# Index scores summed by GpSimd instead of VectorE, and the two short query blocks put in front

## The chip, the cores and the metric

The kernel runs on one core of one Trainium2 chip. The metric is the device time of one execution in microseconds. A core has a tensor engine (PE), VectorE (DVE), ScalarE (ACT), GpSimd (POOL) and SyncE (SP), which issues transfers; each takes its own instructions in order, and they meet only at semaphores.

## The reference, cut to what matters

Two transformer layers on 1024 tokens of width 1024. The change touches one part of the first: sparse attention with an indexer, beside a banded window attention. For each block of 128 queries:

```python
dots  = einsum('bqhd,bsd->bqhs', iq, ik) * 64 ** -0.5        # 8 index heads
score = einsum('bqh,bqhs->bqs', iw, relu(dots))              # summed over the heads
score = where(key_pos <= t, score, -1e30)
_, idx = top_k(score, 256)                                   # 256 keys of each query
logits = ql . c_kv[idx] + bias;  p = softmax(logits);  o = p . c_kv[idx]   # 8 heads
```

Block b sees (b + 1) x 128 keys. Blocks 0 and 1 have at most 256 and need no selection.

## The kernel before, in words

The attention stage is a list of slots (n, i), A_SLOTS: n counts query blocks in the order of ORDER, i the eight heads. In slot g = 8n + i every engine does its part of a pipeline: the tensor engine the logits of g + 1, the transposes of g - 1 and the values of g - 2; VectorE the bias and the maximum of g; ScalarE the exponentials of g. `shared_jobs` adds smaller products that share psum banks, at their places in a slot: window attention of block n + 1 (`a_log` in slots 0 to 3, `a_t`, `a_out`), the index dots of block n + 2 (`ix`, one slot ahead of their sum), the latent queries, the output of block n - 1 in slot 2, and the 24 modulation products of the second layer (`ada`, 1 MB of weights each, loaded by SyncE into two buffers).

The selection for a block is a search by bits for the 256th score, 32 rounds on VectorE. Round 0 (`pick_side`) chooses the side by the sign, each of the next 31 (`pick_bit`) counts the scores above a limit over the whole row (line 1997), compares the count (1999) and changes a bit of the limit (2002); the last one is followed by `pick_mask`, eight wider operations, of which three wide ones (scan, product, difference) take two tensors. The tensor engine adds the mask to the logits, so the first logits of a block wait for it. `pick_rounds` says which rounds stand in which slot; the first half of them comes before the window scores (`window_scores`, line 2046) and the reciprocal of the slot's exponentials (2111), the second behind.

Before the change the order is 1, 7, 6, 5, 4, 3, 2, 0. VectorE also sums the index heads (`index_sum`, lines 2077 and 2080): one operation per head, which multiplies a head's dots by its weight and adds them. Two buffers RL hold the dots of two heads. Block 7, the first with a selection, has its 32 rounds in the 15 slots from (-1, 0) to (0, 6); later blocks have 4 in each slot from (n - 2, 7) to (n - 1, 6). GpSimd makes the causal fill (`causal`, 2691) and multiplies the window's exponentials by their reciprocals (2701).

Of the kernel before, what the change touches and what calls it, by code (L numbers as in the profile page):

```python
# [16 lines left out]
P = 128  # L17
# [6 lines left out]
NH = 8  # L24
# [49 lines left out]

ORDER = (1, 7, 6, 5, 4, 3, 2, 0)
A_SLOTS = [(n, i) for n in range(-1, NT + 1) for i in range(NH) if NH * n + i <= NH * NT + 2]
BITS = 32
FIRST_ROUNDS = (2,) * 13 + (3, 3)
PLACES = ("first", "out", "query0", "banded", "ix0", "ix1", "turned", "ada", "query1")
# [6 lines left out]

ADA_SLOTS = [(-1, i) for i in (1, 3, 5, 7)] + [(0, i) for i in range(NH)] + [(n, i) for n in range(1, 7) for i in (4, 5)]


def pick_rounds(n, i):  # L90

    g = NH * n + i + NH
    if g < len(FIRST_ROUNDS):
        a = sum(FIRST_ROUNDS[:g])
        return 1, a, a + (FIRST_ROUNDS[g] + 1) // 2, a + FIRST_ROUNDS[g]
    m, r = (n + 2, 0) if i == NH - 1 else (n + 1, 4 * i + 4)
    return (m, r, r + 2, r + 4) if picking(m) else None


def shared_jobs(n, i):  # L100

    m, k, h, jobs = n + 1, n + 2 + (i + 1) // NH, (i + 1) % NH, {}
    if i == 2 and n >= 1:
        jobs["first"] = ("d_out", n - 1)
    if i == 7 and 0 <= m < NT:
        jobs["out"] = ("a_out", m, 0)
    if i < 3 and 0 <= n < NT:
        jobs["out"] = ("a_out", n, i + 1)
    if 0 <= m < NT and i < 4:
        jobs["banded"] = ("a_log", m, i)  # L110
    if 0 <= m < NT and i >= 6:
        jobs["turned"] = ("a_t", m, i - 6)
    if i < 2 and 0 <= n < NT:
        jobs["turned"] = ("a_t", n, i + 2)
    if k >= 2 and picking(k):
# [23 lines left out]

EARLY_BANKS, LATE_BANKS, EARLY_END, LATE_AT = (7, 5, 3), (7, 5, 3), 7, 5 * NH + 1  # L140
U_BANK, U_AT, U_COUNT, U_EARLY = {}, {}, {3: 0, 5: 0, 7: 0}, {}
# [11 lines left out]
def build_program(nc, I, out):  # L153
    with ExitStack() as ctx:
# [529 lines left out]
        def _(pe):  # L684
# [151 lines left out]
            pe.wait_ge(f_free, FT["memT"])  # L836
            b = ORDER[1]
            for h in range(NH):
# [76 lines left out]
            def sparse_logits(g):  # L915
                n = g // NH
                freed(("query", n, 0))
                freed(("query", n, 1))
                if g == NH + 1:
                    pe.wait_ge(u_free[3], U_EARLY[3])  # L920
                if g >= 2:
                    pe.wait_ge(s("d_e"), g - 1)
                else:
                    pe.wait_ge(s("ix0_e"), NH - 1 + g)
                L = (ORDER[n] + 1) * P
                if picking(n):
                    pe.wait_ge(s("picked"), n)
                for a in range(0, L, BW):
                    z = min(L, a + BW)
                    o = PS[:, 2 * (g % 2) + a // BW, 0:z - a]  # L930
                    ins = pe.matmul(o, lhsT=QL[:, g % NH, :], rhs=cT[:, a:z], start=True, stop=not picking(n))
                    if picking(n):
                        ins = pe.matmul(o, lhsT=ident_h[:, :], rhs=MSK[:, n % 2, a:z], start=False, stop=True)
                ins.then_inc(s("d_l"), 1)

            def sparse_transposes(g):
                pe.wait_ge(s("d_n"), g + 1)
                if g >= 1:
                    pe.wait_ge(s("d_te"), g)
                if g == NH:  # L940
                    pe.wait_ge(u_free[5], U_EARLY[5])
# [405 lines left out]
        def _(act):  # L1347
# [157 lines left out]
            def empty_shared(job):  # L1505
# [18 lines left out]
                elif kind == "ix":  # L1524
                    k, h, c = job[1:]
                    a, z = BW * c, min((ORDER[k] + 1) * P, BW * c + BW)
                    i = NH * (k - 1) + h
                    if i >= 2:
# [8 lines left out]

            L = (ORDER[1] + 1) * P
            for h in range(NH):
# [329 lines left out]
        def _(dve):  # L1869
# [125 lines left out]
            def pick_bit(b, w, v):  # L1995
# [5 lines left out]
                if b > 0:  # L2001
                    mark(dve.scalar_tensor_tensor(limit_i, limit_i, 1 << (b - 1), over_i, ALU.bitwise_xor, ALU.bitwise_xor))
                else:
                    mark(dve.tensor_tensor(limit_i, limit_i, over_i, ALU.bitwise_xor))

            def pick_mask(m, w, v):
# [11 lines left out]
                settled()  # L2018
                if m >= 3:
                    dve.wait_ge(s("d_l"), NH * (m - 1))  # L2020
                dve.tensor_tensor(MSK[:, m % 2, 0:w], above[:, 0:w], equal[:, 0:w], ALU.subtract).then_inc(s("picked"), 1)

            def pick(m, first, last):
# [3 lines left out]
                for i in range(first, last):  # L2027
                    if i == 0:
                        dve.wait_ge(s("ix_c"), m)
                    settled()  # L2030
# [35 lines left out]

            def index_sum(k, h):
                b = ORDER[k]
                L, i = (b + 1) * P, NH * (k - 1) + h
                if k == 1:  # L2070
                    dve.wait_ge(s("ix0_e"), h + 1)
                else:
                    for c in range((L - 1) // BW + 1):
                        job = ("ix", k, h, c)
                        dve.wait_ge(u_free[U_BANK[job]], U_AT[job] + 1)
                if h == 0:
                    dve.tensor_scalar(score[:, k % 2, 0:L], RL[:, 0, 0:L], iwt[:, b, 0:1], None, ALU.mult).then_inc(s("ix_s"), 1)
                else:
                    dve.wait_ge(s("ix_s"), i)
                    dve.scalar_tensor_tensor(score[:, k % 2, 0:L], RL[:, h % 2, 0:L], iwt[:, b, h:h + 1], score[:, k % 2, 0:L],  # L2080
                                             ALU.mult, ALU.add).then_inc(s("ix_s"), 1)

            for h in range(NH):
                index_sum(1, h)
            dve.wait_ge(s("attn_in"), 16 * 7)
            mark(dve.tensor_tensor(bias[:, NH:2 * NH, :], bias[:, NH:2 * NH, :], over_last(far, 2 * P), ALU.subtract))
            settled()
            for n, i in A_SLOTS:
# [8 lines left out]
                if 0 <= g < NH * NT:  # L2097
                    dve.wait_ge(s("d_lb"), g + 1)
                    dve.tensor_reduce(nmd[:, i:i + 1], pair, AX.X, ALU.max, negate=True).then_inc(s("d_m"), 1)
                if n >= 0 and picking(n + 2):  # L2100
                    index_sum(n + 2, i)
                if i == 4 and 0 <= m < NT:
# [546 lines left out]
        def _(pool):  # L2649
# [38 lines left out]
            def causal(m):  # L2688
                pool.wait_ge(s("ix_s"), NH * m)
# [4 lines left out]
            causal(1)  # L2694
            for m in range(NT):
                if m >= 2 and picking(m):
                    causal(m)
# [183 lines left out]
```

## Time and profile before

| | us |
|---|---|
| median of 3 runs | 3418.36 (3418.05 to 3422.99) |
| the profiled execution: its time | 3422.59 |
| its span, first to last instruction | 3420.8 |
| tensor engine busy | 3109.7 (91%) |
| VectorE busy | 1399.1 (41%) |
| ScalarE busy | 918.0 (27%) |
| GpSimd busy | 815.5 (24%) |

Shares over the whole span mix stages with different limits; they say little on a change in one stage. The page's 40 slices show the attention stage: from about 250 to 780 us VectorE's digit is 8 or 9, elsewhere 1 to 5. The rows below are of that stage.

### The profile page before, as it was taken

The page shows a single profiled execution, that of the slowest core. Times are in us where ns is not written, and L with a number is a line of the kernel's source. Part 1 is how long each engine was busy: PE and PEld are TensorE (multiplying, and loading weights), DVE is VectorE, ACT ScalarE, POOL GpSimd, SP SyncE. Part 2 cuts the span into 40 slices and gives each one's busy share as a digit, 9 for nine tenths or more (in the row PEclk, how much of TensorE's full clock was granted, in tenths as well). Part 3 has the DMA queues.
Part 4 walks back from the last instruction along what each step waited for, and adds up shares of the span by engine and source line. Part 5 has one row for each costly group of instructions (what it writes and reads, how often), then busy time and mean ns, then how long its engine had stood idle before and what let it go on. Part 6 is the DMA issues. An engine that isn't in the chain of part 4 may idle for free. (4 is left out here: it accounts for less than half of the span.)

```text
span 3420.8 us, 40871 instructions
## 1 busy us (share of the span) xinstructions
PE 3109.7 (91%) x16622; PEld 2516.2 (74%) x16622; DVE 1399.1 (41%) x2837; ACT 918.0 (27%) x1571; POOL 815.5 (24%) x330
## 2 busy tenths in 40 slices
PE   5987888876799979999999989999969999999997
PEld 4864555556768878888888847888759788888886
DVE  4048888963421453222222354123553432222226
ACT  3223444452222221111111142014431411211211
POOL 3110000004211133333333333231111222322223
PEclk9996888898999989999999999999989999999999
DMA  5223101011131111111111131100031121111112
GB/s 128 65 75 112 46 18 38 26 39 62 63 104 37 26 56 38 49 49 49 49 49 49 37 132 50 50 28 15 15 105 50 50 56 50 49 49 47 44 45 98
DMA packets 178761, 187.76 MB, mean 55 GB/s; under 512 B 24732, under 2 KB 147484, under 8 KB 178237
## 3 DMA queue, kind: packets, MB, share of 16 engines
q1 hardware_dynamic: 169696, 174.05, 16.4%
q10 hardware_dynamic: 8924, 11.74, 1.0%
q8 instruction: 100, 1.64, 0.2%
q14 instruction: 41, 0.33, 0.0%
HBM read 172.09 MB, written 13.68 MB: 54 GB/s over the span
## 5 line engine op out<-in xcount | busy, mean ns | idle before, releaser
L2659 POOL TENSOR_TENSOR weights_parts<-weights,weights_parts 128x2048 fp32r<-128x2048 f32 (+3 forms) x97 | 436.4, 4499 | 1159.1 <-ACT weights_parts L1369 1159.1
L732 PE MATMUL psum<-x_cols_parts,weights_parts 128*128 128x512 f32 x1552 | 609.0, 392 | 23.4 <-POOL weights_parts L2659 13.2
L734 PE MATMUL psum<-x_cols_parts,weights_parts 128*128 128x512 f32 x1552 | 607.2, 391 | 0.0
L734 PE MATMUL psum<-weights_parts,region_parts 128*128 128x512 f32 (+1 forms) x1120 | 410.2, 366 | 0.0
L732 PEld LDWEIGHTS psum<-x_cols_parts,weights_parts 128*128 128x128 f32 x1552 | 293.8, 189 | 87.5 <-issue 12.0
L732 PE MATMUL psum<-weights_parts,region_parts 128*128 128x512 f32 x864 | 337.4, 391 | 6.9 <-DVE region_parts L2613 5.8
L734 PEld LDWEIGHTS psum<-x_cols_parts,weights_parts 128*128 128x128 f32 x1552 | 293.5, 189 | 61.3
L1369 ACT ACTIVATE weights_parts<-weights 128x2048 fp32r<-128x2048 f32 (+2 forms) x98 | 181.8, 1855 | 580.8 <-DMA region<-in_bup_h_dram 142.6
L733 PE MATMUL psum<-weights_parts,region_parts 128*128 128x512 f32 x864 | 337.1, 390 | 0.0
L732 PE MATMUL psum<-weights_parts,x_cols_parts 128*128 128x256 f32 (+1 forms) x832 | 241.1, 290 | 29.5 <-POOL wide_parts L2706 12.3
L733 PE MATMUL psum<-wide_parts,weights_parts 128*128 128x512 f32 x616 | 241.0, 391 | 0.0
L733 PE MATMUL psum<-weights_parts,x_cols_parts 128*128 128x256 f32 (+1 forms) x832 | 240.1, 289 | 0.0
L734 PEld LDWEIGHTS psum<-weights_parts,region_parts 128*128 128x128 f32 x1120 | 212.6, 190 | 34.0
L732 PEld LDWEIGHTS psum<-weights_parts,region_parts 128*128 128x128 f32 x864 | 162.9, 189 | 41.5 <-DVE region_parts L2613 6.3
L733 PEld LDWEIGHTS psum<-weights_parts,region_parts 128*128 128x128 f32 x864 | 162.8, 188 | 33.8
L732 PEld LDWEIGHTS psum<-weights_parts,x_cols_parts 128*128 128x128 f32 x832 | 162.5, 195 | 30.9 <-issue 21.8
L733 PE MATMUL psum<-extra_parts,weights_parts 128*128 128x512 f32 x456 | 178.9, 392 | 0.0
L1997 DVE TENSOR_SCALAR_CACHE_REDUCE rows<-x_cols,rows 128x1024 bf16<-128x1024 f32 (+5 forms) x186 | 175.0, 941 | 3.3
L2236 DVE TENSOR_TENSOR x_rows<-x_rows,psum 128x512 f32<-128x512 f32 x112 | 77.0, 687 | 212.1 <-PE psum L734 212.1
L733 PEld LDWEIGHTS psum<-weights_parts,x_cols_parts 128*128 128x128 f32 x832 | 162.6, 195 | 0.0
L734 PE MATMUL psum<-weights_parts,wide_parts 128*128 128x256 f32 (+1 forms) x544 | 156.8, 288 | 0.0
L2602 DVE TENSOR_SCALAR region<-region 128x1024 f32<-128x1024 f32 x22 | 17.9, 815 | 318.4 <-ACT region L1846 305.0
(371 smaller groups left out, 5171.2 us busy)
## 6 DMA issues: line engine op xcount, KB each, us to landing
weights<-in_ada_w_dram SPq DMA_DIRECT2D x24, 1024.0 KB, 5.2
weights<-in_ffn_up_w_dram SPq DMA_DIRECT2D x42, 512.0 KB, 4.5
weights<-in_w_up_dram SPq DMA_DIRECT2D x16, 1024.0 KB, 5.1
weights<-in_w_down_dram SPq DMA_DIRECT2D x16, 1024.0 KB, 5.0
weights<-in_m_in_w_dram SPq DMA_DIRECT2D x12, 1024.0 KB, 5.3
weights<-in_ffn_down_w_dram SPq DMA_DIRECT2D x10, 1024.0 KB, 5.1
weights<-in_xa_wkv_dram SPq DMA_DIRECT2D x4, 2048.0 KB, 8.2
weights<-in_m_in_w_dram SPq DMA_DIRECT2D x3, 2048.0 KB, 8.3
```

Of the source, the lines that this page charges most:

```text
L732: pe.matmul(o, lhsT=a_hi, rhs=b_hi, start=(first and i == 0), stop=False)
L733: pe.matmul(o, lhsT=a_hi, rhs=b_lo, start=False, stop=False)
L734: m = pe.matmul(o, lhsT=a_lo, rhs=b_hi, start=False, stop=(last and i == len(terms) - 1))
L1369: act.activation(WHI[buf][:, 0:width], WRAW[buf][:, 0:width], ACT.Copy).then_inc(s("w_hi"), 1)
L1997: mark(dve.tensor_scalar(above[:, 0:w], v, limit, None, ALU.is_ge, ALU.add, accum_out=cnt))
L2236: dve.tensor_tensor(v, v, PS[:, 4 + (TT["down"] + m) % 4, :], ALU.add).then_inc(t_free, 1)
L2602: dve.tensor_scalar(dst, src, k[:, 1:2], k[:, 3:4], ALU.mult, ALU.add).then_inc(s("taps"), 1)
L2659: pool.tensor_tensor(WLO[buf][:, 0:width], WRAW[buf][:, 0:width], WHI[buf][:, 0:width], ALU.subtract).then_inc(s("w_lo"), 1)
```

## The change

GpSimd sums the index heads of blocks 6 to 2, in two operations per head (a multiplication in place in RL, then an addition); VectorE keeps those of block 7. The order becomes 1, 0, 7, 6, 5, 4, 3, 2. Block 7's rounds spread over 23 slots, one in each of block -1, two in each of block 1 and in the first of block 0, then one. Later blocks' rounds stand in slots (n - 1, 0) to (n - 1, 6), as 5, 5, 5, 5, 4, 4, 4, and none in slot 7. The modulation products move to slots of n = -1, 0, 1 and 6. The bit step of a round becomes an operation with one tensor and a pointer to one number.

```diff
-ORDER = (1, 7, 6, 5, 4, 3, 2, 0)
+ORDER = (1, 0, 7, 6, 5, 4, 3, 2)
+FIRST = 2
-FIRST_ROUNDS = (2,) * 13 + (3, 3)
+ROUNDS = (5, 5, 5, 5, 4, 4, 4, 0)
+FIRST_ROUNDS = (1,) * 8 + (2,) * 9 + (1,) * 6
-ADA_SLOTS = [(-1, i) for i in (1, 3, 5, 7)] + [(0, i) for i in range(NH)] + [(n, i) for n in range(1, 7) for i in (4, 5)]
+ADA_SLOTS = sorted([(n, i) for n in (-1, 1) for i in (1, 3, 5, 7)] + [(n, i) for n in (0, 6) for i in range(NH)])
...
-        return 1, a, a + (FIRST_ROUNDS[g] + 1) // 2, a + FIRST_ROUNDS[g]
-    m, r = (n + 2, 0) if i == NH - 1 else (n + 1, 4 * i + 4)
-    return (m, r, r + 2, r + 4) if picking(m) else None
+        return FIRST, a, a + (FIRST_ROUNDS[g] + 1) // 2, a + FIRST_ROUNDS[g]
+    m, a = n + 1, sum(ROUNDS[:i])
+    return (m, a, a + (ROUNDS[i] + 1) // 2, a + ROUNDS[i]) if picking(m) else None
...
-EARLY_BANKS, LATE_BANKS, EARLY_END, LATE_AT = (7, 5, 3), (7, 5, 3), 7, 5 * NH + 1
+EARLY_BANKS, LATE_BANKS, EARLY_END, LATE_AT = (7, 5, 3), (7, 5, 3), FIRST * NH - 1, 6 * NH + 1
...
-                    mark(dve.scalar_tensor_tensor(limit_i, limit_i, 1 << (b - 1), over_i, ALU.bitwise_xor, ALU.bitwise_xor))
+                    mark(dve.tensor_scalar(limit_i, limit_i, 1 << (b - 1), over_i, ALU.bitwise_xor, ALU.bitwise_xor))
...
-                if n >= 0 and picking(n + 2):
-                    index_sum(n + 2, i)
...
+            def index_sum(k, h):
+
+                b = ORDER[k]
+                L, at = (b + 1) * P, NH * (k - FIRST) + h
+                v, u = score[:, k % 2, 0:L], RL[:, h % 2, 0:L]
+                for c in range((L - 1) // BW + 1):
+                    job = ("ix", k, h, c)
+                    pool.wait_ge(u_free[U_BANK[job]], U_AT[job] + 1)
+                if h == 0:
+                    if k >= FIRST + 2:
+                        pool.wait_ge(s("picked"), k - FIRST - 1)
+                    pool.tensor_scalar(v, u, iwt[:, b, 0:1], 0.0, ALU.mult, ALU.add).then_inc(s("ix_s"), 1)
+                else:
+                    pool.tensor_scalar(u, u, iwt[:, b, h:h + 1], 0.0, ALU.mult, ALU.add).then_inc(s("ix_w"), 1)
+                    pool.wait_ge(s("ix_w"), (NH - 1) * (k - FIRST - 1) + h)
+                    pool.wait_ge(s("ix_s"), at)
+                    pool.tensor_tensor(v, v, u, ALU.add).then_inc(s("ix_s"), 1)
...
+            causal(FIRST)
+            for n, i in A_SLOTS:
+                if i == 6 and 0 <= n + 1 < NT:
+                    normalise(n + 1)
+                if n + 2 > FIRST and picking(n + 2):
+                    index_sum(n + 2, i)
+                    if i == NH - 1:
+                        causal(n + 2)
```

## Rows read from the trace of the kernel before

**Rows 1.** Windows: length, busy time of each engine (instructions), clock, DMA share, GB/s

```profile
252.80:347.98 95.18, 69.63 (x828) 42.62 (x828) 84.67 (x188) 35.66 (x105) 8.34 (x4) 0.68 0.34 109
347.98:368.04 20.06, 17.29 (x121) 8.27 (x122) 17.31 (x45) 7.04 (x19) 0.29 (x1) 0.84 0.27 91
368.04:398.43 30.39, 27.26 (x141) 16.22 (x141) 27.43 (x65) 14.94 (x24) 0.00 (x0) 0.95 0.00 1
398.43:440.11 41.68, 32.50 (x253) 20.73 (x252) 35.95 (x76) 20.99 (x46) 3.74 (x2) 0.79 0.16 51
440.11:527.08 86.97, 74.05 (x480) 47.66 (x480) 75.43 (x182) 41.88 (x86) 4.04 (x3) 0.87 0.08 25
602.94:670.57 67.63, 56.86 (x416) 38.21 (x416) 60.62 (x182) 33.51 (x78) 4.35 (x3) 0.85 0.10 32
670.57:724.57 54.00, 39.24 (x352) 27.49 (x352) 50.03 (x176) 27.32 (x70) 4.04 (x3) 0.88 0.12 40
724.57:775.91 51.34, 45.03 (x420) 33.49 (x420) 17.40 (x60) 35.11 (x118) 2.04 (x2) 0.92 0.14 23
```

**Rows 2.** Groups on VectorE: shape and count, busy us, mean ns, idle before

```profile
L2080 DVE SCALAR_TENSOR_TENSOR x_cols<-extra,rows,x_cols 128x1024 f32<-128x1024 f32 (+5 forms) x42 | 44.4, 1057 | 4.4 <-ACT extra L1530 2.3 <-ACT extra L1543 1.7
L1999 DVE TENSOR_SCALAR rows<-rows 128x1 int32<-128x1 f32 x186 | 39.8, 214 | 6.6
L2002 DVE SCALAR_TENSOR_TENSOR rows<-rows 128x1 int32<-128x1 int32 x180 | 31.2, 174 | 6.1
L2077 DVE TENSOR_SCALAR x_cols<-extra,rows 128x1024 f32<-128x1024 f32 (+5 forms) x6 | 3.5, 580 | 37.3 <-ACT extra L1543 33.4 <-ACT extra L1530 3.9
```

**Rows 3.** Groups on VectorE with shapes kept apart, of 1024 columns

```profile
L1997 DVE TENSOR_SCALAR_CACHE_REDUCE rows<-x_cols,rows 128x1024 bf16<-128x1024 f32 x31 | 39.5, 1273 | 0.4
...
L2080 DVE SCALAR_TENSOR_TENSOR x_cols<-extra,rows,x_cols 128x1024 f32<-128x1024 f32 x7 | 9.0, 1284 | 2.1 <-ACT extra L1543 1.7
```

**Rows 4.** Timeline before block 1: start, duration, engine, [idle before and releaser]

```profile
272.33 0.51 ACT L1501 ACTIVATE extra<-extra,rows 128x256 f32<-128x256 f32 x1 [6.93 <-DVE rows L2059]
...
279.69 1.89 POOL L2701 TENSOR_TENSOR extra<-extra,rows 128x1024 f32<-128x1024 f32 x1 [27.06 <-DVE rows L2065]
...
286.90 0.43 DVE L2096 TENSOR_TENSOR psum<-psum,x_cols 128x256 f32<-128x256 f32 x1
...
297.27 0.69 DVE L2046 SCALAR_TENSOR_TENSOR extra<-psum,x_cols 128x512 f32<-128x512 f32 x1 [3.23 <-PE psum L898]
```

**Rows 5.** Timeline behind block 6's mask, slots (1, 7) and (2, 0)

```profile
440.25 1.19 PE L931 MATMUL psum<-region,x_cols 128*128 128x512 f32 x1 [4.15 <-DVE mask_rows L2021]
...
446.84 0.16 DVE L2111 RECIPROCAL rows<-rows 128x1 f32<-128x1 f32 x1 [0.18 <-ACT region L1563]
...
455.39 0.69 DVE L2046 SCALAR_TENSOR_TENSOR extra<-psum,x_cols 128x512 f32<-128x512 f32 x1 [0.72 <-PE psum L872]
```

**Rows 6.** Timeline of slots (1, 4) to (1, 6): modulation products and the reciprocal

```profile
407.59 0.22 ACT L1535 ACTIVATE weights<-psum 128x64 f32<-128x64 f32 x1 [1.19 <-PE psum L905]
...
422.24 1.89 PE L905 MATMUL psum<-weights,cond 128*2 128x64 f32 x64 [0.47 <-ACT extra L1530]
...
430.20 0.16 DVE L2111 RECIPROCAL rows<-rows 128x1 f32<-128x1 f32 x1 [3.00 <-ACT region L1563]
```

**Rows 7.** Timeline of slot (2, 6), where a GpSimd product and a sum meet

```profile
508.33 3.74 POOL L2701 TENSOR_TENSOR extra<-extra,rows 128x1024 f32<-128x1024 f32 x2 [65.26 <-DVE rows L2065]
...
510.25 2.51 DVE L2080 SCALAR_TENSOR_TENSOR x_cols<-extra,rows,x_cols 128x640 f32<-128x640 f32 x1 [0.55 <-ACT extra L1530]
```

**Rows 8.** Groups on GpSimd: two tensors, and one

```profile
L2811 POOL TENSOR_TENSOR region<-region 128x1024 f32<-128x1024 f32 x22 | 52.7, 2394 | 197.9 <-ACT region L1850 192.5 <-ACT region L1834 5.4
...
L2745 POOL TENSOR_SCALAR_AFFINE_SELECT rows<-rows 36x1024 f32<-36x1024 f32 x1 | 1.1, 1087 | 0.1
```

**Rows 9.** Timeline of block 2 without rounds: two slots' maxima

```profile
742.32 0.56 DVE L2099 TENSOR_REDUCE rows<-psum 128x1 f32<-128x384 f32 x1
...
744.91 0.56 DVE L2099 TENSOR_REDUCE rows<-psum 128x1 f32<-128x384 f32 x1
```

More of the change, by code:

```diff
@@ L114, in shared_jobs @@
         jobs["turned"] = ("a_t", n, i + 2)
-    if k >= 2 and picking(k):
+    if k > FIRST and picking(k):
         jobs["ix0"] = ("ix", k, h, 0)
@@ L836, in _ @@
             pe.wait_ge(f_free, FT["memT"])
-            b = ORDER[1]
+            b = ORDER[FIRST]
             for h in range(NH):
@@ L918, in sparse_logits @@
                 freed(("query", n, 1))
-                if g == NH + 1:
+                if g == FIRST * NH + 1:
                     pe.wait_ge(u_free[3], U_EARLY[3])
@@ L926, in sparse_logits @@
                 if picking(n):
-                    pe.wait_ge(s("picked"), n)
+                    pe.wait_ge(s("picked"), n - FIRST + 1)
                 for a in range(0, L, BW):
@@ L939, in sparse_transposes @@
                     pe.wait_ge(s("d_te"), g)
-                if g == NH:
+                if g == FIRST * NH:
                     pe.wait_ge(u_free[5], U_EARLY[5])
@@ L1526, in empty_shared @@
                     a, z = BW * c, min((ORDER[k] + 1) * P, BW * c + BW)
-                    i = NH * (k - 1) + h
+                    i = NH * (k - FIRST) + h
                     if i >= 2:
@@ L1536, in empty_shared @@
                 ins.then_inc(u_free[U_BANK[job]], 1)
-            L = (ORDER[1] + 1) * P
+            L = (ORDER[FIRST] + 1) * P
             for h in range(NH):
@@ L2018, in pick_mask @@
                 settled()
-                if m >= 3:
+                if m >= FIRST + 2:
                     dve.wait_ge(s("d_l"), NH * (m - 1))
@@ L2028, in pick @@
                     if i == 0:
-                        dve.wait_ge(s("ix_c"), m)
+                        dve.wait_ge(s("ix_c"), m - FIRST + 1)
                     settled()
@@ L2065, in window_sum, with first_sum @@
                 dve.reciprocal(den, den).then_inc(s("a_d"), 1)
[L2067 to L2071, printed above, removed]
-                else:
[L2073 to L2081, printed above, removed]
+            def first_sum(h):
+                b = ORDER[FIRST]
+                L, v = (b + 1) * P, score[:, FIRST % 2, 0:(b + 1) * P]
+                dve.wait_ge(s("ix0_e"), h + 1)
+                if h == 0:
+                    dve.tensor_scalar(v, RL[:, 0, 0:L], iwt[:, b, 0:1], None, ALU.mult).then_inc(s("ix_s"), 1)
+                else:
+                    dve.wait_ge(s("ix_s"), h)
+                    dve.scalar_tensor_tensor(v, RL[:, h % 2, 0:L], iwt[:, b, h:h + 1], v, ALU.mult, ALU.add).then_inc(s("ix_s"), 1)
             for h in range(NH):
-                index_sum(1, h)
+                first_sum(h)
             dve.wait_ge(s("attn_in"), 16 * 7)
@@ L2688, in causal @@
             def causal(m):
-                pool.wait_ge(s("ix_s"), NH * m)
+                pool.wait_ge(s("ix_s"), NH * (m - FIRST + 1))
                 v = score[:, m % 2, ORDER[m] * P:ORDER[m] * P + P]
@@ L2692, in causal, with normalise @@
                                    pattern=[[-1, P]], channel_multiplier=1).then_inc(s("ix_c"), 1)
[L2694 to L2697, printed above, removed]
+            def index_sum(k, h):
[5 more added lines that the diff above has]
+                    pool.wait_ge(u_free[U_BANK[job]], U_AT[job] + 1)
+                if h == 0:
+                    if k >= FIRST + 2:
[6 more added lines that the diff above has]
+                    pool.tensor_tensor(v, v, u, ALU.add).then_inc(s("ix_s"), 1)
+            def normalise(m):
                 w0 = P if ORDER[m] == 0 else 0
```

## The prediction

> **What bounds the kernel now.** The page comes first: the tensor engine is busy almost everywhere, but from about 250 to 780 us its share dips and VectorE's stands at 8 or 9 tenths. That is the attention stage, all that the diff touches, so only there can time change; behind it the same work follows. I cut the stage where a mask is finished, because the tensor engine waits there for VectorE [rows 1]. From block 7's mask on, VectorE is busy for 27.43 of 30.39 us in slots 1 to 3 and 35.95 of 41.68 in slots 4 to 6. But the tensor engine is busy for 27.26 of the same 30.39, so the second limit lies close behind. After the last mask (724.57 to 775.91) VectorE works only 17.40 of 51.34 us, and the tensor engine sets the pace. The timelines then show who waits for whom inside a slot.
>
> **VectorE's work.** Five blocks' sums leave it: 35 sums (the 42 less block 7's seven: 44.4 - 9.0 = 35.4) and five first products (3.5 less one of 0.8), so 38.1 us [rows 2, 3]. The bit step of 180 rounds becomes one operation with a pointer. The nearest row is line 1999, 214 ns where line 2002's plain two-tensor form takes mostly 160 (174 with its delays); I take 0.055 us x 180 = 10 us more, with 0 and 10 as ends. Block 0, now in front of the last mask, brings about 8 (eight biases and maxima at 0.6, and 3.4 for a set of window scores). Net, VectorE has 38 - 10 - 8 = 20 us less before the last mask. Whether that is time depends on the waits.
>
> **The start.** A round of block 7 is 1.27 + 0.21 + 0.17 us and small gaps, 1.77 [rows 2, 3]; with the pointer 1.82. Between 252.80 and 347.98 (95.18 us) lie 32 of them and block 1. Eight leave the first stretch. What comes next there is a chain: window maximum, exponentials (from 272.33), GpSimd's normalisation (279.69), transposes; the first logits reach VectorE at 286.90 [rows 4]. Of the 14.6 us from the exponentials on, some 2.8 were rounds between the exponentials' end and the window's sum, so the bare chain is 11.7; the maximum ends 6.5 us earlier, at 265.8 (four of the eight rounds before it fall away, 7.1 us, less the pointers and a short wait for the last score). Block 1's slot 0 thus starts at 277.5, 9.4 us earlier, not 14. It then waits for the tensor engine: the window scores came 10.4 us after the slot's start (297.27, with 3.23 of waiting), 3.3 of them index dots that move away, so now 7.1, at 284.6. The rest of slot 0 is 2.5. Three slots of two rounds follow at 5.0 (2 x 1.82 + 0.9 + 0.6), then 7.1 with the window maximum (2.3 and three small steps), 4.6, 7.1 and 5.4 (4.6 each, with 2.5 and 0.7 of waits for the latent query's copy, which ScalarE makes before it turns to the exponentials): block 1 ends at 326.3. Block 0's slots have one round, but the dots, their copies and the window jobs of block 7 need 4.3 to 5.0 us on the tensor engine: 19.3 for slots 0 to 3. Slot 4 is 5.4, slot 5 3.7, and slot 6 0.6 + 1.8 + a mask of 7.3 + 4 us in which GpSimd is in the way (below). Block 7's mask is done at 368.4 instead of 347.98: **+20.4**.
>
> The modulation products bring their loads (1 MB each, on SyncE's queue, two buffers, 5.2 us from issue to landing by the page). With two in flight a product every 5 us, as in block 1's slots, is served; behind them on that queue only the first output weights wait, and the last product now ends some 17 us before they are used.
>
> **A block between two masks, for block 7.** First slot 7 and slot 0. Slot 7 now has no rounds. After a mask the tensor engine, which had waited 4.15 us, takes the next logits, then the window output; ScalarE copies that before slot 7's exponentials, so the reciprocal comes 6.7 us after the mask (440.11 to 446.84) [rows 5]. VectorE's own work there is 1.7 us; what filled the other 5 were rounds. That cover is gone, and what is late next is slot 0's scores. They came 15.3 us after the mask, and VectorE had waited 0.72 for them. New: 6.8 + 1.6 + 2.2 + two rounds, 14, still under 15.3. So the pair keeps its 20.06 us and gives nothing, but three rounds more than before lie behind it.
>
> Slots 1 to 3 take five rounds instead of four and no sum: one round of 896 columns (1.63) and five pointers (0.28) less a sum of 768 (1.05) = +0.86 in a slot where VectorE never waited, and +0.1 where it waited 0.7 to 1.1 (slots 1, 2): 30.39 becomes 31.4, **+1.05**.
>
> Slots 4 to 6 lose a sum each, but the reciprocal of slot 6 already waited 3.00 us [rows 6]. Its chain runs through the tensor engine. Modulation product 4 delays the window exponentials by 1.2 (ScalarE waited 1.19 for it), and product 5 took 1.89 at the lower clock in front of the logits. Both leave this block, less 0.2 of overlap: **-2.85**. The sums themselves give nothing more.
>
> **GpSimd in the mask.** A 128x640 sum on VectorE that met a GpSimd product of two tensors took 2.51 us, where one of 1024 columns takes 1.28 [rows 3, 7]. The new bit step has one tensor, but the mask with the last bit still has five operations of two tensors, and GpSimd now runs head 7's product and sum beside it. GpSimd's price: two tensors cost 2394 ns for 1024 columns, one pass over one tensor 1087 (line 2745) [rows 8], so for 896 columns 2.1 + 0.95 with the near row, 4.2 with the far one. Slots there are 8 us and more: hidden. In block 0's slots 4.2 would add up to 0.5 a slot, 4 us. In slot 6 the normalisation comes first in GpSimd's order and waits for VectorE's window sum; behind it stand heads 6 and 7 and the causal fill, and for those the sign step of the next block, which comes only in slot 0: they have over 10 us, so that wait costs nothing. Each mask meets one or two such operations: +2.0, 1.8, 1.6, 1.4 for the blocks that have sums beside them, with 0 and 6 as ends.
>
> By the Trainium skill (SBUF — State Buffer, "SBUF: two separate sides") the port is an exclusive lock for the whole instruction, and VectorE's one-tensor operations in a two-port mode take part in it too. No row of before shows the second half; by it the mask's two comparisons, and the sign step, would wait as well, which would put the price at its upper end.
>
> **The sum.** Block 7: +1.05 - 2.85 + 2.0 = +0.2, and 0.1 in its first pair: +0.3. Blocks 6, 5 and 4 (86.97 us the first, 67.63 the last of the three [rows 1]) worked the same way: +0.3, +1.05, -0.4; the smaller the block, the less a sum was worth and the less it waited. Block 3 has no sums before or after, but three slots with one round more (1.10 and five pointers, +1.38 each), and eight modulation products, of 1.07 us at the full clock, where it had two; most lie beside VectorE's rounds, so 0.7 more, and 0.3 less in the first pair: +4.5 on 54.00. After the last mask block 2 stands alone, without windows, dots and products, and block 0 is gone. Slot 7 and slot 0 take 7.9 with the product; slots 1 to 3 have outputs and transposes left, 3.3 + 3.6 + 2.3; the bare ones 2.1, from 2.59 with a window job of 0.5 [rows 9]: 7.9 + 9.2 + 8.4 = 25.5, and 1.3 more of drain than block 0 had, against 51.0: **-24.2**.
>
> 20.4 + 0.3 + 0.3 + 1.05 - 0.4 + 4.5 - 24.2 = +2.0 us against the profiled execution (3422.59, span 3420.8). The median is 3418.36, so **3420**. What VectorE is relieved of comes back as idle time of VectorE: slot 7 of six blocks, and block 0's slots.
>
> **Rivals.** *VectorE is the only bound* and the waits stay as they are: -20 before the last mask, -24 behind it, 3374; with half of the new waits filled 3397. For it: 85 to 95% busy. Against it: slot 7's reciprocal needs the tensor engine's output 6.7 us after the mask whatever VectorE does. 0.22. *The port (slower):* all eight wide operations of a mask queue behind GpSimd, which also normalises in slot 6, at 1.9 us each. GpSimd has some 9 us of work there, so at most 7 of delay per mask; from 3.5 us a mask on it decides: 5 x 7 - 11 = +24, 3444. For it: the 2.51 us row. Against it: part of GpSimd's work is over before the mask begins. 0.16. *GpSimd holds up block 0:* at the far price its two operations become the slot, +8, 3428; for it, no row has the one-tensor form; 0.07. My own case has 0.55, with 3411 to 3430.
>
> A measurement of this kernel tells about 0.2%, 7 us, from no change. From my case 0.41 is within it, 0.10 slower, 0.04 faster; nearly all of the first rival is faster, 0.21 and 0.01; the port is slower; the third splits. Faster 0.25, same 0.46, slower 0.29. The range reaches toward half of the first rival and half of the port: 3400 to 3438.
>
> **What the new profile should show.** Last mask near 751, last slot's maximum near 777. Reciprocals of slot 7 waiting about 5 us for ScalarE in blocks 7 to 3. Line 2002 at about 214 ns. The two GpSimd operations near 0.95 and 2.1 us for 896 columns. Block 7's mask ready about 20 us later than now. The forecast is wrong if slot 7 doesn't idle (the tensor engine faster after a mask), if the bit step costs 160 ns, or if masks grow by more than 3 us.

## The result, and the profile after

The changed kernel takes 3427.69 us (median of 10, 3423.22 to 3434.66), the kernel before 3420.62 in the same group (10, 3417.78 to 3426.16). The ratio is 1.002, 95% interval 1.0011 to 1.003: about 7 us slower. The forecast was 3420, with 3400 to 3438 as range and 0.2% as the bound of what can be told; the result lies inside the range and on that bound. The profiled execution took 3425.77 (span 3424.0), 3.2 above the one of before.

The windows from one mask to the next, which answer to [rows 1]; the last ends at the last slot's maximum:

```profile
252.80:366.90 114.10, 90.50 (x1204) 59.31 (x1204) 91.48 (x215) 53.08 (x177) 31.70 (x22) 0.78 0.42 137
366.90:458.67 91.77, 74.50 (x371) 42.58 (x376) 75.14 (x176) 41.62 (x86) 28.48 (x20) 0.86 0.04 12
458.67:546.02 87.35, 72.10 (x348) 45.96 (x352) 72.54 (x175) 41.22 (x84) 21.66 (x18) 0.85 0.00 1
546.02:625.55 79.53, 64.80 (x308) 42.15 (x312) 63.53 (x174) 36.77 (x76) 18.48 (x18) 0.82 0.00 1
625.55:693.67 68.12, 54.48 (x284) 36.55 (x288) 58.63 (x174) 33.20 (x76) 15.82 (x18) 0.85 0.00 1
693.67:751.43 57.76, 43.95 (x665) 32.38 (x672) 50.54 (x174) 28.44 (x75) 3.75 (x2) 0.88 0.35 111
751.43:776.96 25.53, 25.20 (x228) 18.28 (x228) 8.88 (x25) 17.51 (x47) 0.00 (x0) 0.90 0.26 44
```

Between the first and the last mask VectorE worked 320.4 of 384.5 us; before it was 334.2 of 376.6. It was relieved of 14 us there, and the stretch grew by 8. Up to the last mask, block 0's slots in front included, VectorE's busy time fell by only 7.3 us:

```profile
0.00:724.57 724.57, 584.85 (x4036) 408.45 (x4036) 486.93 (x1225) 291.37 (x603) 88.06 (x46) 0.87 0.22 63
```

```profile
0.00:751.43 751.43, 604.50 (x4188) 424.82 (x4212) 479.63 (x1219) 307.31 (x672) 178.30 (x123) 0.88 0.21 61
```

The timeline at slot 7 of blocks 7 to 4, where VectorE waits for ScalarE's exponentials (block 3's row says 3.62):

```profile
372.44 0.16 DVE L2105 RECIPROCAL rows<-rows 128x1 f32<-128x1 f32 x1 [4.94 <-ACT region L1565]
465.10 0.16 DVE L2105 RECIPROCAL rows<-rows 128x1 f32<-128x1 f32 x1 [4.82 <-ACT region L1565]
552.12 0.16 DVE L2105 RECIPROCAL rows<-rows 128x1 f32<-128x1 f32 x1 [4.63 <-ACT region L1565]
631.01 0.16 DVE L2105 RECIPROCAL rows<-rows 128x1 f32<-128x1 f32 x1 [4.13 <-ACT region L1565]
```

Groups: the bit step, and GpSimd's sum and product at 896 columns:

```profile
L2004 DVE TENSOR_SCALAR rows<-rows 128x1 int32<-128x1 int32 x180 | 38.5, 214 | 6.3
L2704 POOL TENSOR_TENSOR x_cols<-x_cols,extra 128x896 f32<-128x896 f32 x7 | 15.2, 2168 | 0.6
L2701 POOL TENSOR_SCALAR extra<-extra,rows 128x896 f32<-128x896 f32 x7 | 7.5, 1072 | 17.4 <-ACT extra L1532 17.4
```

Block 7's last bit step and mask in the kernel before (VectorE), then in the changed kernel (VectorE, then GpSimd beside it):

```profile
340.48 0.16 DVE L2004 TENSOR_TENSOR rows<-rows 128x1 int32<-128x1 int32 x1
...
341.54 0.81 DVE L2011 TENSOR_SCALAR rows<-x_cols,rows 128x1024 bf16<-128x1024 f32 x1
342.38 1.22 DVE L2013 TENSOR_SCALAR_CACHE_REDUCE rows<-rows 128x1024 bf16<-128x1024 bf16 x1
343.64 2.35 DVE L2015 TENSOR_TENSOR_SCAN rows<-rows 128x1024 bf16<-128x1024 bf16 x1
...
347.29 0.69 DVE L2021 TENSOR_TENSOR mask_rows<-rows 128x1024 bf16<-128x1024 bf16 x1
```

```profile
355.89 1.84 DVE L2006 TENSOR_TENSOR rows<-rows 128x1 int32<-128x1 int32 x1
...
358.63 1.52 DVE L2013 TENSOR_SCALAR rows<-x_cols,rows 128x1024 bf16<-128x1024 f32 x1
360.18 1.22 DVE L2015 TENSOR_SCALAR_CACHE_REDUCE rows<-rows 128x1024 bf16<-128x1024 bf16 x1
361.45 2.78 DVE L2017 TENSOR_TENSOR_SCAN rows<-rows 128x1024 bf16<-128x1024 bf16 x1
...
365.52 1.38 DVE L2023 TENSOR_TENSOR mask_rows<-rows 128x1024 bf16<-128x1024 bf16 x1
```

```profile
353.98 3.75 POOL L2711 TENSOR_TENSOR extra<-extra,rows 128x1024 f32<-128x1024 f32 x2 [1.89 <-DVE rows L2067]
358.59 1.02 POOL L2701 TENSOR_SCALAR extra<-extra,rows 128x896 f32<-128x896 f32 x1 [0.86 <-ACT extra L1532]
359.69 2.39 POOL L2704 TENSOR_TENSOR x_cols<-x_cols,extra 128x896 f32<-128x896 f32 x1
364.96 1.41 POOL L2701 TENSOR_SCALAR extra<-extra,rows 128x896 f32<-128x896 f32 x1 [2.88 <-ACT extra L1532]
```

Three of VectorE's wide operations there each meet a GpSimd operation and take 0.4 to 0.7 us longer. The last bit step, an operation of one column with two tensors, takes 1.84 us for 0.16: it ends at 357.73, with the window's normalisation on GpSimd. From the first wide comparison to the mask's end the masks of blocks 7 to 2 take 9.05, 7.25, 6.86, 5.15, 4.29 and 3.56 us; before the change 7.23, 6.51, 5.76, 5.04, 4.29 and 3.57. The wide operations thus pay 1.8 + 0.7 + 1.1 + 0.1 = 3.8 us. From the last bit step on, as the forecast counted its two-tensor operations, the masks take 11.01, 7.52, 7.64, 5.91, 5.36 and 3.84 us; before, 7.50, 6.78, 6.03, 5.31, 4.56 and 3.84. GpSimd's price in the masks is 3.5 + 0.7 + 1.6 + 0.6 + 0.8 = 7.3 us (with rounding), nearly half of it in operations of one column.

### The profile page after: what moved, and what is told of

Its sections match the earlier page's. It is cut to its first block and busy times, and to the rows that moved or that the text cites. A ratio compares the mean times of both kernels' runs of the same rounds, so it can differ in the third digit from the quotient of the medians.

```text
span 3424.0 us, 40905 instructions
## 1 busy us (share of the span) xinstructions
PE 3111.6 (91%) x16598; PEld 2518.8 (74%) x16622; DVE 1383.1 (40%) x2797; ACT 917.8 (27%) x1571; POOL 904.2 (26%) x405
## 5 line engine op out<-in xcount | busy, mean ns | idle before, releaser
L1999 DVE TENSOR_SCALAR_CACHE_REDUCE rows<-x_cols,rows 128x1024 bf16<-128x1024 f32 (+5 forms) x186 | 175.0, 941 | 3.2
L1636 ACT ACTIVATE region<-psum,region 128x512 f32<-128x512 f32 x64 | 44.2, 690 | 386.2 <-PE psum L736 386.2
```

Source lines behind the costliest of these rows:

```text
L1636: act.activation(RU[:, m % 4, :], PS[:, (FT["up"] + m) % 4, :], ACT.Relu, bias=upb[:, m // 4, (m % 4) // 2:(m % 4) // 2 + 1]).then_inc(f_f ...
L1999: mark(dve.tensor_scalar(above[:, 0:w], v, limit, None, ALU.is_ge, ALU.add, accum_out=cnt))
```

## The experiments

Ratios are against the kernel before in the same group. "Slot 7" says whether the later blocks' rounds begin there.

| kernel | slot 7 | sums | order | ratio (95%) | median |
|---|---|---|---|---|---|
| changed | no | GpSimd | new | 1.0020 (1.0011 to 1.0030) | 3427.7 |
| 1 | no | VectorE | new | 1.0030 (1.0019 to 1.0041) | 3434.6 |
| 2 | yes | GpSimd | new | 0.9954 (0.9942 to 0.9966) | 3407.8 |
| 9, the same again | yes | GpSimd | new | 0.9957 (0.9943 to 0.9971) | 3404.1 |
| 5 | yes | VectorE | new | 0.9995 (0.9986 to 1.0004) | 3423.0 |
| 11 | yes | GpSimd | old | 1.0008 (0.9999 to 1.0017) | 3424.8 |
| 12 | yes | VectorE | old | 1.0010 (1.0001 to 1.0019) | 3425.0 |

All seven have the new bit step; the products stand as in the changed kernel where the order is new, and as before where it is old.

**1. Sums back on VectorE.** One operation per head again, behind the slot's maximum; GpSimd keeps `causal` alone. The removed line is in GpSimd's list, the added ones are in VectorE's.

```diff
                 if n + 2 > FIRST and picking(n + 2):
-                    index_sum(n + 2, i)
                     if i == NH - 1:
...
+                if n + 2 > FIRST and picking(n + 2):
+                    index_sum(n + 2, i)
                 if i == 4 and 0 <= m < NT:
```

> The changed kernel with the index sums of blocks 6 to 2 back on VectorE, one operation per head (38.1 us of work on VectorE come back); order, rounds, products and bit step stay. My theory (tensor engine and ScalarE set slot 7, block 0's slots and part of slots 1, 2 and 6; the sums lie beside them): the eight sums of block 6 stand in block 0's slots and cost nothing, those of slots 7 and 6 cost nothing, the 24 of slots 0 to 5 of four blocks cost some 0.9 each less 6 us of waits, and masks and rounds get back some 7 us that GpSimd took from them: about +9 us against the changed kernel, 3437. Rival, VectorE is the only bound: +38 less 7, 3459. Rival, the port costs more than the sums are worth: below the changed kernel, 3420 or less.

Measured: 0.1% over the changed kernel's ratio, 3.4 us, with some 5 of uncertainty. The masks are back at 7.23, 6.50, 5.76 and 5.03 us, and the last bit steps at 0.16. "VectorE is the only bound" (+38 - 7) falls. With slot 7 empty the move of 38 us of work is worth nothing that can be told.

**2 and 9. Rounds from slot 7 on.**

```diff
-    m, a = n + 1, sum(ROUNDS[:i])
-    return (m, a, a + (ROUNDS[i] + 1) // 2, a + ROUNDS[i]) if picking(m) else None
+    m, a = (n + 2, 0) if i == NH - 1 else (n + 1, 4 * i + 4)
+    return (m, a, a + 2, a + 4) if picking(m) else None
```

> The changed kernel with the later blocks' rounds as before the change, four in each slot from slot 7 on; all else as changed. My theory: slot 7's idle time of VectorE (4.9, 4.8, 4.6, 4.1 and 3.6 us by the profile after) takes the four rounds, the pair of slots 7 and 0 keeps its length, and slots 1 to 3 of five blocks have a round less: 3 x (1.6 + 1.5 + 1.3 + 1.2 + 1.0) = 20 us, less some 3 of new waits: about -17 against the changed kernel, 3411, which would be below both kernels. Rival, the rounds were hidden in slots 1 to 3 (the tensor engine sets them): -3 to +1. Rival, GpSimd's last sum and causal fill come too late for slot 7's rounds, so that VectorE waits there in front of the reciprocal: slot 7 grows by up to 5 us a block, +5 to +20.

> The same kernel as the second run (the changed kernel with later blocks' rounds from slot 7 on), once more, beside the others of this group: its first interval rested on six executions. My theory: 0.9954 within 0.001, so 3406 to 3409 where the kernel before has 3422. Rival, it was a lucky group: 0.998 and over.

Measured: 0.9954 and 0.9957, 15 us below the kernel before and 22 below the changed one. Both beat both kernels. Windows of run 2 from block 7's mask to the last, from there to the last slot's maximum, then to the end:

```profile
366.66:728.74 362.08, 296.49 (x1976) 192.95 (x2000) 316.69 (x868) 181.22 (x397) 88.20 (x76) 0.89 0.07 21
728.74:753.46 24.72, 24.36 (x228) 17.54 (x228) 8.89 (x27) 17.52 (x47) 0.00 (x0) 0.93 0.27 45
753.46:3400.20 2646.74, 2481.50 (x12184) 2076.34 (x12182) 894.82 (x1554) 593.04 (x852) 726.06 (x282) 0.97 0.16 53
```

The stretch between the masks is 22.5 us shorter than in the changed kernel, with nearly the same work on VectorE (316.7 for 320.4) and GpSimd. Block 7's slot 7 in the timeline:

```profile
369.08 1.08 DVE L1988 TENSOR_SCALAR_CACHE_REDUCE rows<-x_cols 128x896 bf16<-128x896 f32 x1 [1.82 <-issue]
...
372.93 0.15 DVE L2105 RECIPROCAL rows<-rows 128x1 f32<-128x1 f32 x1
```

The third theory was right in small: VectorE waits 1.82 us there for the causal fill behind GpSimd's last sum. But the wait lies inside the one for ScalarE, and the reciprocal has no wait left. From the start of slot 7's maximum to that of slot 1's it is 18.9 us here, 19.2 in the changed kernel, 20.1 before. The five pairs of slots 7 and 0 (from the end of one maximum to that of the other) take 81.5, 82.1 and 83.4 us: in these three kernels the pair's length hardly depends on its rounds.

The 22.5 us came back in two places. Slots 1 to 3 of the five blocks went from 140.9 to 127.2 us, which is where a round was taken out; slots 4 to 6, which have four rounds a slot in both kernels, went from 162.0 to 153.8. In block 7's slots 4 to 6 the reciprocals wait 1.4 us for ScalarE here and 4.8 in the changed kernel; what shortened these waits was not traced. Run 9's profile shows the same split, with 130.3 and 153.5 us.

**3. The bit step with two tensors again.**

```diff
-                    mark(dve.tensor_scalar(limit_i, limit_i, 1 << (b - 1), over_i, ALU.bitwise_xor, ALU.bitwise_xor))
+                    mark(dve.scalar_tensor_tensor(limit_i, limit_i, 1 << (b - 1), over_i, ALU.bitwise_xor, ALU.bitwise_xor))
```

> The changed kernel with the bit step of the 180 rounds as two-tensor operation again. Its plain time is 159 ns, the new form's 214. Before the change its mean was 174 with GpSimd's 28 us of normalisation beside the rounds; with some 90 us of GpSimd operations beside them three times that delay, 45 ns, so the mean should be about 205 and the time as that of the changed kernel, -2 us (3426). Rival, GpSimd does not hold it up: mean near 165, -8 to -10 us, 3418. Rival, each one that meets a GpSimd operation waits half of it or more: mean of 300 ns and over, +15 us.

Measured: 1.0007 (0.9998 to 1.0016), 4 us below the changed kernel, with as much uncertainty. Group of the bit step:

```profile
L2004 DVE SCALAR_TENSOR_TENSOR rows<-rows 128x1 int32<-128x1 int32 x180 | 42.1, 234 | 6.1
```

158 of the 180 take 0.16 us, 22 take 0.17 to 1.71. The two-tensor form does wait behind GpSimd, by 75 ns in the mean (I expected 45).

**4. Products back in slots 4 and 5.**

```diff
-ADA_SLOTS = sorted([(n, i) for n in (-1, 1) for i in (1, 3, 5, 7)] + [(n, i) for n in (0, 6) for i in range(NH)])
+ADA_SLOTS = [(-1, i) for i in (1, 3, 5, 7)] + [(0, i) for i in range(NH)] + [(n, i) for n in range(1, 7) for i in (4, 5)]
```

> The changed kernel with the modulation products in their old slots (4 and 5 of the blocks n = 1 to 6, all of n = 0, the odd ones of n = -1). My theory: in blocks 7, 6, 5 and 4 slots 4 to 6 lengthen by 2.85 us each, block 0's slots lose four products (-2 to -4) and block 3 loses six (-1): +6 to +9 against the changed kernel, 3435. Rival, the products were hidden in both places: 0 within 2 us.

Measured: 1.0023 (1.0012 to 1.0034), the changed kernel's time within 1 us, though single executions went up to 3446.7. The median speaks for the rival: moving the products was worth nothing that can be told.

**5. Rounds from slot 7 on, and the sums on VectorE.** The edits of 1 and 2 together.

> The changed kernel with both undone: later blocks' rounds from slot 7 on, and the sums of blocks 6 to 2 on VectorE (new order, products and bit step stay). The run with rounds in slot 7 alone gave 3407.8, 16 us below the kernel before; the run with the sums on VectorE alone gave +3 against the changed kernel. My theory: with slot 7 filled VectorE has no idle cover left, so here the sums' place counts: 28 sums outside block 0's and sixth slots at 0.9, less 6 us of waits and 7 that GpSimd took, +12 against 3407.8, 3420. Rival, the sums are worth as little as they were with slot 7 empty: +3, 3411. Rival, VectorE alone sets the time: +31, 3439.

Measured: 0.9995, 14 us above run 2, as my theory had it. Here the place of the sums counts. Window between the masks:

```profile
371.22:745.81 374.59, 300.92 (x1984) 195.13 (x2006) 339.22 (x901) 181.51 (x399) 21.55 (x15) 0.88 0.06 21
```

Of the 22.5 us of VectorE that GpSimd takes over there in run 2, 12.5 become time, 2.5 of them in the first pair of slots 7 and 0 (22.3 for 19.9 us), with the tensor engine at a lower clock behind the mask (0.64 for 0.97 in its first 8 us). Another 4.6 come ahead of block 7's mask (371.22 for 366.66), but 2.5 of these are there already in block 7's round 0 (its sign step starts at 257.29 for 254.82), and up to that point the two kernels do the same.

**6. Rounds from slot 7 on, old order** (new product slots kept).

```diff
-ORDER = (1, 0, 7, 6, 5, 4, 3, 2)
-FIRST = 2
+ORDER = (1, 7, 6, 5, 4, 3, 2, 0)
+FIRST = 1
...
-FIRST_ROUNDS = (1,) * 8 + (2,) * 9 + (1,) * 6
+FIRST_ROUNDS = (2,) * 13 + (3, 3)
...
-EARLY_BANKS, LATE_BANKS, EARLY_END, LATE_AT = (7, 5, 3), (7, 5, 3), FIRST * NH - 1, 6 * NH + 1
+EARLY_BANKS, LATE_BANKS, EARLY_END, LATE_AT = (7, 5, 3), (7, 5, 3), FIRST * NH - 1, 5 * NH + 1
```

> The kernel with GpSimd's sums, the new bit step and the new product slots, later blocks' rounds from slot 7 on, and the old block order 1, 7 to 2, 0 with block 7's rounds as (2 x 13, 3, 3). Against the run with rounds in slot 7 and the new order (3407.8). My theory: the order alone moves block 0's slots from behind the last mask to a place in front of the first and is nearly a wash: block 7's mask comes 19 us sooner, the part behind the last mask is 24 us longer, +5, and block 6's sums stand in block 1's slots: +5, 3413. Rival, block 0 in front gives room for 23 slots of rounds and the old order loses that: +20. Rival, the old order is better by the mask that comes sooner: -5 or more.

Measured: 0.9996 (0.9987 to 1.0005), 14 us above run 2, not 5. The window behind the last mask says that the run is not clean:

```profile
719.97:777.61 57.64, 51.69 (x804) 39.49 (x804) 17.57 (x59) 36.63 (x124) 2.04 (x2) 0.93 0.46 131
```

Eight products stand there in the old order, where the tensor engine sets the pace: 57.6 us for 51.3. Run 11 takes them away.

**7. Rounds from slot 7 on, bit step with two tensors.** The edits of 2 and 3.

> The run with rounds in slot 7 (3407.8), and the bit step as two-tensor operation. With GpSimd's sums beside it this form took 234 ns in the mean (159 free of them), the other 214: +3.6 us of work on VectorE in 180 rounds. My theory, VectorE's slots are the bound here: +2 to +4, 3411. Rival: the plain form's 159 ns in block 7's first rounds, where no sums run, outweigh it: -2, 3406.

Measured: 0.9975 (0.9965 to 0.9986), 6 to 7 us above runs 9 and 2 by the ratios. The form's mean was 250 ns, so some 6 us more of VectorE's work. But this does not show that the delays cost time. In the profile 5.0 of the difference lie in one place, the pair of slots 7 and 0 behind block 7's mask, at half clock here and at full clock in run 2:

```profile
364.71:372.71 8.00, 7.05 (x18) 3.97 (x18) 3.13 (x12) 1.98 (x4) 3.38 (x3) 0.50 0.01 2
365.31:390.11 24.80, 20.59 (x130) 11.16 (x132) 16.97 (x43) 7.93 (x22) 5.35 (x6) 0.78 0.14 43
```

```profile
366.66:374.66 8.00, 6.24 (x32) 2.90 (x37) 5.86 (x20) 2.94 (x9) 3.13 (x3) 0.97 0.00 0
367.25:387.10 19.85, 16.53 (x117) 8.54 (x118) 16.95 (x44) 6.38 (x19) 4.03 (x5) 0.85 0.17 54
```

VectorE works the same 17.0 us in both. The difference of the ratios is barely outside their uncertainty.

**8. GpSimd's last two heads held behind the mask.**

```diff
                 v, u = score[:, k % 2, 0:L], RL[:, h % 2, 0:L]
+                if h >= 6:
+                    pool.wait_ge(s("picked"), k - FIRST)
```

> The changed kernel with GpSimd's products and sums of heads 6 and 7 held until the mask of slot 6 is finished; the window's normalisation stays where it was. In the changed kernel the five masks that have sums beside them took 3.75 us more in sum than before the change (9.05, 7.25, 6.86, 5.15 and 4.29 us for 7.23, 6.51, 5.76, 5.04 and 4.29). My theory: those 3.75 us go where the sums caused them and stay where the normalisation did; block 7's mask 7.2 to 8.0 us, block 6's 6.5 to 7.3, block 5's 5.8; the time falls by 0 to 4 us, 3424 to 3428. Rival, the sums held back make ScalarE's next copy and the causal fill late, and slot 7 and slot 0 grow: +3 to +10.

Measured: 1.0005 (0.9995 to 1.0014), 5 us below the changed kernel, barely outside the uncertainty. From the first wide comparison the masks take 7.23, 6.51, 5.76, 5.03, 4.30 and 3.57 us: that lengthening came from the two heads' operations. The last bit step of block 7 still takes 1.84 us (from 356.93, while the normalisation runs from 355.02 to 358.77). So 1.7 of the 7.3 us are the normalisation's and 5.6 the two heads'. In runs 1 and 5, where VectorE still sums, the last bit comes 3.4 us behind the normalisation's end and takes 0.16. Behind block 7's mask the reciprocal waited 10.77 us, with the tensor engine at half clock; runs 7 and 10, which hold nothing, show the same long pair. Block 7's last bit step and mask, timeline:

```profile
356.93 1.84 DVE L2006 TENSOR_TENSOR rows<-rows 128x1 int32<-128x1 int32 x1
...
365.43 0.69 DVE L2023 TENSOR_TENSOR mask_rows<-rows 128x1024 bf16<-128x1024 bf16 x1
366.22 1.01 POOL L2703 TENSOR_SCALAR extra<-extra,rows 128x896 f32<-128x896 f32 x1 [7.46 <-DVE mask_rows L2023]
```

**10. Block 7's rounds moved into VectorE's waits,** with the edit of 2.

```diff
-FIRST_ROUNDS = (1,) * 8 + (2,) * 9 + (1,) * 6
+FIRST_ROUNDS = (1,) * 8 + (3,) + (1,) * 7 + (3, 2, 4, 2, 1, 1, 1)
```

> The run with rounds in slot 7, and block 7's 32 rounds spread as 8 x 1, 3, 7 x 1, 3, 2, 4, 2, 1, 1, 1 instead of 8 x 1, 9 x 2, 6 x 1: out of block 1's slots 1 to 7, into slots (0,0), (1,0), (1,2) and (1,3), where VectorE waited 3.4, 3.8, 3.9 and 1.1 us for window scores. My theory: block 1's slots of 4.6 us shrink until the tensor engine fills them (it was idle for 0 to 1.7 us in them, at either clock), perhaps 0.8 each, and half of it is lost in the slots that take the rounds: -3 against the second run, block 7's mask near 363 us instead of 366.7. Rival, VectorE sets block 1's slots: -10. Rival, the tensor engine sets both blocks: 0, or +2 by rounds in front of scores that are then ready.

Measured: 0.9973 (0.9962 to 0.9985), 5 to 7 us above runs 9 and 2 by the ratios, with some 6 of uncertainty. Block 1's slots 1 to 3 shrank from 4.6 us to 2.9, so there VectorE did set the pace, but block 0's slots grew, block 7's mask came at 369.4, and behind it slot 7 took 14.0 us instead of 9.8. Windows of this run, then of run 2, around the mask:

```profile
353.00:357.00 4.00, 0.66 (x2) 0.44 (x3) 0.46 (x4) 3.78 (x17) 2.23 (x2) 0.50 0.01 2
...
369.00:373.00 4.00, 4.00 (x13) 2.59 (x14) 1.00 (x4) 1.20 (x3) 1.85 (x2) 0.50 0.00 0
```

```profile
349.00:353.00 4.00, 0.13 (x1) 0.13 (x1) 2.43 (x9) 4.00 (x18) 2.77 (x2) 0.66 0.07 24
...
367.00:371.00 4.00, 3.82 (x16) 1.51 (x16) 2.07 (x8) 0.96 (x5) 1.89 (x2) 1.00 0.00 0
```

In both the tensor engine pauses for some 4 us ahead of block 7's mask, waiting for ScalarE's exponentials. In run 2 it was at half clock (0.50, the 1.2 GHz level) from there to about 359 and at full clock behind the mask; here at half clock from 345 to 377, through the work that follows the mask.

**11. Old order with the old product slots.** The edits of 2, 4 and 6: sums on GpSimd and the new bit step are all that is left of the change.

> The sums' move alone, nearly: old block order, old first rounds, old product slots, rounds from slot 7 on, GpSimd's sums and the new bit step. The run with the old order and the new product slots gave 0.9996, and its part behind the last mask lasted 57.6 us (51.3 before the change), because eight products stood there. My theory: with two products there it is 51 to 52 again, -6, and slots 4 and 5 of four blocks get +1 to +2 in sum: ratio 0.998, 3417. Rival, the old order was not at fault at all and the products were: 0.9955, 3406. Rival, the products cost the same wherever they are: 0.9996.

Measured: 1.0008, against an expected 0.998. From the first mask to the last slot's maximum the profiled execution took 366.6 + 50.0 us (run 12: 374.8 + 51.4), so 9.6 us fewer, but 1.3 of them went ahead of the first mask, and behind the attention stage, where nothing differs, it took 5 us more than run 12's. The medians of 11 and 12 are equal; whether the sums' move is worth 0 or up to 5 us in the old order stays open. Nor was my account of run 6 borne out: its last window is back at 50.0 us here for 57.6, but the ratio is no lower (1.0008 for 0.9996, a difference within the uncertainty).

**12. The kernel before with the new bit step alone.**

> The kernel before with only the bit step of the 180 rounds in its new form. By the profiles its mean there goes from 174 to 214 ns, 7.2 us of work on VectorE. My theory: VectorE is busy for 85 to 90% of these slots and each delay of it is on the path but for what its waits take back: +4 to +6, ratio 1.0015. Rival, it is hidden: 1.000. Rival, +10 (my forecast's price of 0.055 us each, all on the path): 1.003.

Measured: 1.0010 (1.0001 to 1.0019), 3.4 us, the mean 214 ns for 174. My +4 to +6 was a little high.

## Why the forecast held, term by term

Its terms against the two profiles:

| term | forecast | measured |
|---|---|---|
| block 7's mask | +20.4 | +18.9 |
| blocks 7, 6 | +0.3, +0.3 | -0.4, +0.4 |
| block 5 | +1.05 | +3.7 |
| block 4 | -0.4 | +0.5 |
| block 3 | +4.5 | +3.8 |
| behind the last mask | -24.2 | -24.6 |
| sum | +2.0 | +2.3 |

The last term runs to ScalarE's first split of the next weights:

```profile
784.73 1.90 ACT L1371 ACTIVATE weights_parts<-weights 128x2048 fp32r<-128x2048 f32 x1
```

It stood at 782.48 before. The other 0.9 us of the profiled 3.2, and the difference between 3.2 and the medians' 7.1, lie in no term: executions of one kernel differ by 8 to 11 us.

**The start and the end.** Right to 1.5 and 0.4 us; the last mask came at 751.43 (751), the last maximum at 776.96 (777). Block 1 began at 277.99 (277.5), its slots 1 to 3 took 4.6 us (5.0). The 51.0 us from which the last term is taken stand as 51.34 in [rows 1]; with them it would be -24.5.

**Slot 7.** Right, and now shown. "The pair keeps its 20.06 us and gives nothing": 20.1 before, 19.2 after, 18.9 with the rounds put back, by the maxima. What the change loses is the four rounds' place: giving slot 7 its rounds again brings 22 us (runs 2 and 9). In run 2's profile 13.7 of them lie in slots 1 to 3, which lose a round, and 8.2 in slots 4 to 6, which don't; the second part is measured and not explained. The forecast's closing sentence, that what VectorE is relieved of comes back as its idle time in slot 7 and in block 0's slots, was right for slot 7. Block 0's slots are not a loss: the new order, with its places for the products and for block 7's rounds, is worth having once slot 7 is filled and GpSimd sums (0.9954 for 1.0008).

**Slots 1 to 3.** Mis-sized. "+1.05" for each of blocks 7 to 4 and +4.1 for block 3 make some 8 us; measured by the maxima, 127.2 us became 140.9, +13.7; by blocks, 7 to 3, +2.4, +1.1, +5.2, +0.9 and +4.1. With slot 7 filled again it is 127.2 (run 2) and 130.3 (run 9). Most of the miss is block 5's. There slot 2 fell on a half-clock stretch of the tensor engine, which had worked 1.16 us in the 2 before it (568 to 570); two windows and VectorE's wait at that place:

```profile
570.00:574.00 4.00, 4.00 (x16) 3.26 (x16) 3.79 (x11) 0.60 (x1) 1.97 (x2) 0.50 0.00 0
574.00:578.00 4.00, 4.00 (x27) 2.56 (x25) 2.81 (x9) 1.70 (x3) 0.00 (x0) 0.78 0.02 4
```

```profile
580.98 0.69 DVE L2048 SCALAR_TENSOR_TENSOR extra<-psum,x_cols 128x512 f32<-128x512 f32 x1 [3.96 <-PE psum L874]
```

**GpSimd in the mask.** Block 7's 4 us came out at 3.5, but half of it is the last bit step behind the normalisation, 1.7 us. The others were mis-sized the other way: 2.0 + 1.8 + 1.6 + 1.4 make 6.8; measured 3.7. I had each mask meet one or two whole operations; an operation that has begun costs only its rest. Over all, 10.8 became 7.3. The error here and the one in slots 1 to 3 nearly cancel, so that the sum is better than its parts, which is luck. The sign that I named for a wrong forecast, "masks grow by more than 3 us", did appear, in block 7's, where my own sum had 4.

**VectorE's work.** "20 us less before the last mask" was wrong: 486.93 us became 479.63, 7.3 less. The step that failed is that I took the sums off VectorE and put none of GpSimd's delays back. GpSimd's operations lengthened VectorE's by some 13 us in the changed kernel (each against the shortest of its shape in all kernels): 7.3 in the masks, and 5.5 in the small two-tensor operations around the window's maximum, which have eight columns (line 2061 took 2.06 us where its plain time is 0.16, in block 0's slot 4). The sum of times did not use this number, only the first rival did.

**The bit step.** 214 ns as said. Its 10 us were priced against 160 ns; the old form beside GpSimd's sums takes 234 (run 3) or 250 (run 7), so in this kernel the new form takes less of VectorE, not more. Whether this is time is not shown: run 3 was 4 us faster with the old form and run 7 6 to 7 slower, and both have the long pair of slots behind block 7's mask. On the kernel before it costs 3.4 us (run 12).

**GpSimd's prices.** 1.07 and 2.17 us for 896 columns; the near row gave 0.95 and 2.1, the far one 4.2 for the product.

**The products.** "-2.85" a block was not borne out: with the products in their old slots the time is the same within 1 us (run 4). By the profile slots 4 to 6 of five blocks went from 166.2 to 162.0 us, where the forecast's terms came to -4.6 (four times -2.85, and the masks' 6.8); with the masks' 3.7 the rest is -7.9 for -11.4. It was right as a sum only.

**The rivals.** "VectorE is the only bound" would have given 3374, or 3397 with half of the new waits filled. Runs 2 and 9 come part of the way, with 3404 to 3408: there slot 7's waits are filled, and the move of the sums gives 14 us (run 5). The port as the slower rival needed 3.5 us per mask. It got 3.5 in block 7's, from the last bit step on, and 0.9 in the mean of the four others. Its "eight wide operations" are six; the other two records of the mask have one column.

## What to carry to other kernels

Work that stands in an engine's wait can be free, and moving it out is not, as here with slot 7: before rounds are spread anew, look at which slot has a wait that another engine sets, and leave them there. Relieving the busiest engine pays only where no other chain closes behind it: the same 38 us were worth 3 us with slot 7 empty and 14 with it filled, each with some 5 of uncertainty. Parts of a change should be run alone and in pairs, since here, with slot 7 filled, order (with its products) and sums together gave 18 to 19 us and each alone 1 to 5. And a difference of 5 us between two such kernels wants a look at the clock's windows before it is put down to the edit.

## What the hardware showed

GpSimd holds up VectorE's one-tensor operations too, not only those with two. The wide comparison (L2013) took 1.52 us for 0.81 when it met GpSimd's product of 1.02 us. The delay does not shrink with the operation: the last bit step, one column with two tensors, took 1.84 us for 0.16 and ended with the normalisation. It goes both ways: GpSimd's product at 364.96 took 1.41, with VectorE's two-tensor product before it. But the one-tensor operations that also accumulate were never delayed: the count (L1999) has a mean of 941 ns with GpSimd's sums and 941 without (run 1), and the mask's (L2015) took 1.22 beside GpSimd's addition. Nor was the one-column form with a pointer, 214 ns in the mean in every kernel that has it. This is what the Trainium skill (SBUF — State Buffer, "SBUF: two separate sides") says of an exclusive lock, that one-tensor operations in a two-port mode take part as well; the rows agree with it for the comparison, and for block 6's sign step (0.90 us for 0.69, beside a GpSimd product). The conclusion that I drew from it, the upper end of the price (6 us a mask), did not follow: the masks pay 0.6 to 3.5, because few of these operations meet one.

The tensor engine's clock was the second thing. Behind block 7's mask it stood at 0.50 in run 10 and at 1.00 in run 2, and slot 7 took 14.0 and 9.8 us. This divides the kernels of the new order: in the profiles of runs 1, 3, 4, 7, 8 and 10 the 8 us behind that mask are at 0.50, and the pair of slots 7 and 0 takes 24.8 to 26.1 us; in the changed kernel and runs 2, 9 and 5 they are at 0.79, 0.97, 0.79 and 0.64, and it takes 20.1, 19.9, 20.1 and 22.3. The six have different edits, and no run sets the clock by itself, so the clock as the cause of these 5 us is argued and not shown. They are as large as most of the differences between single runs above, those of runs 7 and 10 first of all; what rests on larger ones, the 22 us of slot 7 and the 14 of the sums with it filled, stands. The stages between two masks move by several microseconds with where such a stretch falls (block 7's had a mean clock of 0.86 and 91.8 us in the changed kernel, 0.88 and 86.4 in run 2, 0.83 and 96.8 in run 8), which no sum of instruction times foretells. What of run 10's loss is the clock's and what the rounds' was not told apart.
